# Mixer of a hybrid diffusion step: modulation weights loaded from ScalarE's queue, X and Y tables laid out by step, first inverses scattered earlier

## The reference, cut to what matters

```python
def gated_delta_chunked(q, k, v, g, beta, s0):
    ...
    a_mat = jnp.where(strict, jnp.einsum('bhnik,bhnjk->bhnij', kb, k) * decay, 0.0)
    rhs = jnp.concatenate([v * beta[..., None], kb * jnp.exp(gc)[..., None]], axis=-1)
    sol = lax.linalg.triangular_solve(a_mat + jnp.eye(CHUNK, dtype=jnp.float32), rhs,
                                      left_side=True, lower=True, unit_diagonal=True)
    ...
    def step(S, xs):
        u0_c, w_c, qk_c, qd_c, kd_c, gt_c = xs
        u = u0_c - jnp.einsum('bhck,bhkv->bhcv', w_c, S)
        o = jnp.einsum('bhck,bhkv->bhcv', qd_c, S) + jnp.einsum('bhij,bhjv->bhiv', qk_c, u)
        S = S * gt_c[..., None, None] + jnp.einsum('bhck,bhcv->bhkv', kd_c, u)
        return S, o
```

```python
def modulation(cond, w_ada_l, b_ada_l):
    m = jnp.einsum('nd,de->ne', cond, w_ada_l.astype(jnp.float32)) + b_ada_l.astype(jnp.float32)
    return jnp.split(m[:, None, :], 6, axis=-1)
```

## Time and profile before

| | us |
|---|---|
| median of 3 runs | 1893.29 |
| the runs | 1893.01 to 1895.04 |
| profiled execution, its own time | 1897.15 |
| its span in the profile | 1895.4 |
| busy in the span: PE, DVE, ACT, POOL | 1631.1, 1207.6, 932.4, 242.2 |

### The profile page before, as it was taken

The page is one execution under the profiler, slowest core; times in us unless marked ns, Lnnn a source line. Parts: engine busy times, 40 slices in busy tenths (PEclk is TensorE's granted clock), DMA queues, the critical chain, the costliest instruction groups (busy, mean ns, idle before and its releaser), DMA issues. The chain is left out here.

```text
span 1895.4 us, 32729 instructions
## 1 busy us (share of the span) xinstructions
PE 1631.1 (86%) x11909; PEld 1325.4 (70%) x11910; DVE 1207.6 (64%) x1728; ACT 932.4 (49%) x1438; POOL 242.2 (13%) x361
## 2 busy tenths in 40 slices
PE   3998886799895999999949989789979679999992
PEld 0798675687553888888838986678855468888881
DVE  1478453556346996996664883646654579899664
ACT  2254642233323886886543445323341278888651
POOL 0000035111000111111020000541200011111112
PEclk7899998999896999999969999879999889999996
DMA  8241356654305997997553110665331489999754
GB/s 339 78 151 48 100 153 163 189 178 143 137 34 205 412 405 294 380 408 269 211 218 112 56 48 1 174 197 157 95 129 53 167 304 402 408 397 409 296 198 178
DMA packets 186803, 392.96 MB, mean 207 GB/s; under 512 B 88682, under 2 KB 106114, under 8 KB 161094
## 3 DMA queue, kind: packets, MB, share of 16 engines
q1 hardware_dynamic: 163374, 326.12, 47.7%
q10 hardware_dynamic: 14824, 34.39, 4.6%
q0 software_dynamic: 8496, 30.94, 4.3%
HBM read 345.95 MB, written 45.45 MB: 207 GB/s over the span
## 5 line engine op out<-in xcount | busy, mean ns | idle before, releaser
L2363 DVE TENSOR_TENSOR expert_w_lo<-shared,expert_w_hi 128x2048 fp32r<-128x2048 f32 x192 | 433.4, 2287 | 58.3 <-ACT expert_w_hi L2302 58.3
L2302 ACT ACTIVATE expert_w_hi<-shared 128x2048 fp32r<-128x2048 f32 x192 | 366.5, 1913 | 44.1 <-PEq L146 39.6
L2229 PE MATMUL ps<-expert_w_hi,expert_x_hi 128*128 128x512 f32 x592 | 245.2, 414 | 11.0 <-DVE expert_x_lo L2358 9.2
L2231 PE MATMUL ps<-expert_w_hi,expert_x_lo 128*128 128x512 f32 x592 | 233.2, 394 | 0.0
L2230 PE MATMUL ps<-expert_w_lo,expert_x_hi 128*128 128x512 f32 x592 | 233.1, 394 | 0.0
L2229 PEld LDWEIGHTS ps<-expert_w_hi,expert_x_hi 128*128 128x128 f32 x592 | 113.5, 192 | 42.5 <-issue 12.9
L2231 PEld LDWEIGHTS ps<-expert_w_hi,expert_x_lo 128*128 128x128 f32 x592 | 112.3, 190 | 24.3
L2230 PEld LDWEIGHTS ps<-expert_w_lo,expert_x_hi 128*128 128x128 f32 x592 | 112.8, 191 | 18.7
L2284 PE MATMUL ps<-expert_w_hi,expert_hid_hi 128*128 128x512 f32 x296 | 115.8, 391 | 0.5 <-ACT expert_hid_hi L2337 0.5
L2199 POOL COPY expert_cur_idx<-slot_tokens 128x1 int32 x37 | 48.4, 1307 | 530.2 <-PE ps L2216 530.2
L2285 PE MATMUL ps<-expert_w_lo,expert_hid_hi 128*128 128x512 f32 x296 | 115.3, 390 | 0.0
(11 more groups left out here) (380 smaller groups left out, 3376.7 us busy)
## 6 DMA issues: line engine op xcount, KB each, us to landing
shared<-in_w_up SPq DMA_DIRECT2D x64, 1024.0 KB, 7.4
shared<-in_w_down SPq DMA_DIRECT2D x64, 1024.0 KB, 9.4
shared<-in_w_gate SPq DMA_DIRECT2D x64, 1024.0 KB, 8.3
qkv<-in_w_ada SPq DMA_DIRECT2D x20, 1280.0 KB, 6.1
shared<-in_w_in SPq DMA_DIRECT2D x10, 2048.0 KB, 9.2
y_table<-expert_y ACTq DMA_DIRECT2D x37, 512.0 KB, 8.5
qkvT<-in_w_ada SPq DMA_DIRECT2D x20, 768.0 KB, 8.5
setup_ada_ring<-in_w_ada SPq DMA_DIRECT2D x8, 1024.0 KB, 12.2
```

Source lines behind the costliest of these rows:

```text
L2229: pe.matmul(bank, x_hi[:, at], w_hi[:, j, w], start=(q == 0), stop=False)
L2231: return pe.matmul(bank, x_lo[:, at], w_hi[:, j, w], start=False, stop=(q == KD - 1))
L2302: act.activation(w_hi[:, j, :], raw[:, j, :], ACT.Copy).then_inc(w_hi_done, 1)
L2363: dve.tensor_tensor(w_lo[:, j, :], raw[:, j, :], w_hi[:, j, :].bitcast(F32), ALU.subtract).then_inc(w_lo_done, 1)
```

## The change

Four things change, all in the mixer.

- `load_after` is called by ScalarE at the end of `take(n)`, and no longer by SP. The loads of w_ada go to ScalarE's own DMA queue. Only the load of the first unit stays on SP.
- The tables base_x and base_y are laid out by step, both directions of a step side by side. `x_load` and `y_load` issue two loads of 128 KB each, not four of 64 KB.
- The tables corner and qk_table are laid out so that the two directions of a step can be addressed by one pattern: `bl_load` and `qk_load` issue one load, not two.
- `scatter(0)`, `x_load(0)` and `y_load(0)` come before `base_load(3)`; they came after it.

```diff
-    def load_after(self, sp, n):
+    def load_after(self, act, n):
 
         i = self.of_pair(n)
         if i is not None and i + 1 < len(self.todo):
-            sp.wait_ge(self.done, i + 1)
-            self.load(sp, i + 1)
+            act.wait_ge(self.done, i + 1)
+            self.load(act, i + 1)
...
+        def both(table, s, size):
+
+            a, b = (place(ORDER.index(t), d) for d, t in enumerate(tiles(s)))
+            return table[0:2 * NT * size].rearrange("(f x) -> f x", x=size)[a:b + 1:b - a]
...
+        def entry(table, at, n=1):
+
+            return table[at * BASE:(at + n) * BASE]
...
                 def bl_load(s):
                     sp.wait_ge(s_["t1l_p"], s)
-                    for d in range(2):
-                        sp.dma_start(flat(BtL)[half(d)], A.corner[place(s, d), half(d)]).then_inc(s_["bl_in"], 16)
+                    sp.dma_start(flat(BtL), both(A.corner, s, HB * DH * HB).rearrange("f (r n) -> f r n", r=HB)).then_inc(s_["bl_in"], 16)
...
-                    for d in range(2):
-                        sp.dma_start(QK[:, d].rearrange("p h n -> p (h n)"),
-                                     A.qk_table[place(s, d), :, d * DH * P:(d + 1) * DH * P]).then_inc(s_["qk_in"], 16)
+                    sp.dma_start(QK.rearrange("p d h n -> p d (h n)"), paired(both(A.qk_table, s, P * DH * P))).then_inc(s_["qk_in"], 16)
 
                 def scatter(i):
                     sp.wait_ge(s_["inv_done"], group(i) + 1)
                     p = rows_of(i)
                     for d in range(2):
-                        sp.dma_start(small(A.base_x, i, d), (Rt if d else R)[p, d]).then_inc(base_out[group(i)], 16)
-                        sp.dma_start(small(A.base_y, i, d), (R if d else Rt)[p, d]).then_inc(base_out[group(i)], 16)
+                        at = 2 * step_of(i, d) + d
+                        sp.dma_start(small(entry(A.base_x, at)), (Rt if d else R)[p, d]).then_inc(base_out[group(i)], 16)
+                        sp.dma_start(small(entry(A.base_y, at)), (R if d else Rt)[p, d]).then_inc(base_out[group(i)], 16)
 
                 def x_load(s):
...
-                    for d in range(2):
-                        for b in range(2):
-                            sp.dma_start(X[half(b), d], large(A.base_x, place(s, d), b)[:, d * DH:(d + 1) * DH]).then_inc(s_["xy_in"], 16)
+                    for b in range(2):
+                        sp.dma_start(eight_of(X, b), large(entry(A.base_x, 2 * s, 2), b)).then_inc(s_["xy_in"], 16)
...
                     if i + 1 < FRONT:
                         front_out(i + 1)
+                        if i == 2:
+                            scatter(0)
+                            x_load(0)
+                            y_load(0)
                         base_load(i + 1)
-                    units.load_after(sp, i)
-                    if i == 2:
-                        scatter(0)
-                        x_load(0)
-                        y_load(0)
                     units.store_after(sp, i)
                 for s in range(NT):
                     m = FRONT + PER * s
-                    units.load_after(sp, m)
                     if s < 2:
...
-                    units.load_after(sp, m + 1)
                     units.store_after(sp, m + 1)
...
                     act.wait_ge(s_["pt_p"], n + 1)
                     act.activation(pT[:, :, 0:nk], G.ps[:, 6:8, 0:nk], ACT.Copy).then_inc(s_["pt_taken"], 1)
+                    units.load_after(act, n)
```

More of the change, by code:

```diff
@@ L50 @@
 NB = P // SB
-BASE = 2 * 4 * 2 * (HB * HB + HB)
+BASE = 4 * 2 * (HB * HB + HB)
 BASE_PAD = 11 * P * 256
@@ L1149, in mixer_phase, with place, mine, small @@
         blocks = lambda b, c=0: G.ps[:, b, 256 * c:256 * (c + 1)].rearrange("p (h n) -> p h n", h=DH)
[L1151 to L1157, removed]
-            return of.rearrange("e (r n) -> r e n", n=HB)
+        def place(i, d):
+            g = group(i)
+            first, n = (0, 1, 3)[g], (1, 2, 2)[g]
+            return 2 * first + d * n + i - first
+        def both(table, s, size):
+            a, b = (place(ORDER.index(t), d) for d, t in enumerate(tiles(s)))
+            return table[0:2 * NT * size].rearrange("(f x) -> f x", x=size)[a:b + 1:b - a]
+        def mine(table, i, size):
+            return table[0:2 * NT * size].rearrange("(f x) -> f x", x=size)[place(i, 0):place(i, 1) + 1:place(i, 1) - place(i, 0)]
+        def entry(table, at, n=1):
+            return table[at * BASE:(at + n) * BASE]
+        def small(of):
+            of = of.rearrange("(q x) -> q x", x=SB * HB + SB)[:, 0:SB * HB]
+            return of.rearrange("q (r n) -> q r n", n=HB)[:, :, 0:SB]
+        def large(of, b):
+            of = of.rearrange("(e c x) -> e c x", c=2, x=HB * HB + HB)[:, b, 0:HB * HB]
+            return of.rearrange("e (r n) -> r e n", n=HB)
+        def step_of(i, d):
+            t = ORDER[i]
+            return NT - t if d and t else t
+        def paired(of):
+            return of.rearrange("f (p n) -> p f n", p=P)
         eight_of = lambda a, b: a[half(b)].rearrange("p d h n -> p (d h) n")
@@ L1176, in base_load @@
                         sp.wait_ge(s_["inv_done"], 1)
-                    sp.dma_start(V[rows_of(i), 0], small(A.base_b, i, 0)).then_inc(base_in[group(i)], 16)
-                    sp.dma_start(W[rows_of(i)], small(A.base_b, i, 1)).then_inc(base_in[group(i)], 16)
+                    sp.dma_start(V[rows_of(i), 0], small(entry(A.base_b, 2 * i))).then_inc(base_in[group(i)], 16)
+                    sp.dma_start(W[rows_of(i)], small(entry(A.base_b, 2 * i + 1))).then_inc(base_in[group(i)], 16)
                     if i:
@@ L1190, in bt_load @@
                     for d in range(2):
+                        i = ORDER.index(tiles(s)[d])
                         for b in range(2):
-                            sp.dma_start(Bt[half(b), d], large(A.base_b, place(s, d), b)[:, d * DH:(d + 1) * DH]).then_inc(s_["bt_in"], 16)
+                            sp.dma_start(Bt[half(b), d], large(entry(A.base_b, 2 * i + d), b)).then_inc(s_["bt_in"], 16)
                 def bl_load(s):
                     sp.wait_ge(s_["t1l_p"], s)
-                    for d in range(2):
-                        sp.dma_start(flat(BtL)[half(d)], A.corner[place(s, d), half(d)]).then_inc(s_["bl_in"], 16)
+                    sp.dma_start(flat(BtL), both(A.corner, s, HB * DH * HB).rearrange("f (r n) -> f r n", r=HB)).then_inc(s_["bl_in"], 16)
                 def qk_load(s):
@@ L1223, in y_load @@
                         sp.wait_ge(s_["yf_done"], at(s - 1, 1))
-                    for d in range(2):
-                        for b in range(2):
-                            sp.dma_start(Y[half(b), d], large(A.base_y, place(s, d), b)[:, d * DH:(d + 1) * DH]).then_inc(s_["xy_in"], 16)
+                    for b in range(2):
+                        sp.dma_start(eight_of(Y, b), large(entry(A.base_y, 2 * s, 2), b)).then_inc(s_["xy_in"], 16)
                 sp.dma_start(sinks[:, :], A.sink[l:l + 1, :].to_broadcast([P, NH])).then_inc(s_["par_in"], 16)
@@ L1264, in _ @@
                         sp.dma_start(A.new_state[0, l:l + 1].rearrange("a d h k v -> k (a d) h v"), S[:, 0]).then_inc(s_["s_out"], 16)
-                    units.load_after(sp, m + 2)
                     if s + 1 < NT:
@@ L1454, in _ @@
                             else:
-                                pe.wait_ge(s_["xy_in"], 128 * (s + 1))
+                                pe.wait_ge(s_["xy_in"], 64 * (s + 1))
                                 if s:
@@ L1481, in _ @@
                     if s:
-                        pe.wait_ge(s_["bl_in"], 32 * s)
+                        pe.wait_ge(s_["bl_in"], 16 * s)
                     for h in range(DH):
@@ L1519, in _ @@
                     if s:
-                        pe.wait_ge(s_["qk_in"], 32 * s)
+                        pe.wait_ge(s_["qk_in"], 16 * s)
                     if s + 1 == NT:
```

14 lines of the change are left out of this document (6 added, 8 removed).

## The result

The changed kernel takes 1916.67 us (median of 4 runs, 1912.5 to 1918.63) against 1893.15 us (4 runs), a ratio of 1.0119 [1.0101, 1.0138]: +22.5 us [19.1, 26.1], where the forecast was -4.3. The mixer of layer 0 went from 240.2 to 267.0 us (+26.8; forecast +12.2), that of layer 1 from 220.1 to 216.0 us (-4.1; forecast -17.5), both from SP's load of the sinks to its load of o_norm. So both layers miss in the same direction, by 14.6 and 13.4 us. Of layer 0's +26.8 us, TensorE's idle time in the mixer is 17.7 (64.0 against 46.3 us) and its busy time 9.1 (203.0 against 193.9), at a granted clock of 0.87 against 0.92.

What follows compares the result with a forecast made beforehand. TensorE's mixer was taken as a chain with holes, mostly waits for w_ada. Layer 0 +12.2 and layer 1 -17.5 gave -5.3 us, taken as -4.3: from 1893.3 to 1889.0 us, range 1879 to 1900.

Steps and rivals of the forecast that it cites:

- What bounds the kernel: Mixer: a chain on TensorE with holes; largest entry in layer 0 is waits for w_ada, 16.2 us in six.
- The first part: Tables by step, half the loads, earlier scatter(0): holes before steps close, -6.9 and -2.1 us in layer 0.
- bl_load and qk_load save one issue each. The bytes are the same: SP's table loads: one issue fewer for each of the two, with unchanged bytes; no cost given to the new layout.
- The second part: w_ada issued by ScalarE after take(n): later landings open holes in layer 0; pair 5 gains, -2.6 us there.
- the landing: Time from issue to arrival of w_ada's second half: 7.5 us for pairs 11, 14, 17; 9.1 for 6, 9, 10.
- The hole closes: Step 0 of layer 0: tables land at 290.1, before TensorE arrives at 291.0; -6.9 us and -2.1 of clock.
- Rival 3: Step 0: small stores ahead of the scatter cause the delay, so 3 to 4 us stay; 1896 us, chance 0.08.
- The clock: Behind new holes at pairs 9, 11, 14, 17 of layer 0 the granted clock falls: 2.0 us each, +8.0.
- rival 2: The clock stays up in layer 0's new holes of 3.3 to 3.7 us: 1881 us, chance 0.15.
- Rival 1: ScalarE starts the DMA only after the take ends, and every w_ada load takes 9.1 us: 1899 us, chance 0.22.
- Rival 4: Later w_ada loads don't show because TensorE arrives late anyway; layer 0's +25 us losses vanish: 1866 us, chance 0.05.
- pair 10's -2.0: Products of pair 10, layer 0: w_ada lands at 375.4 against 377.41, since SP was late there; -2.0 us.

Runs made afterwards that it cites:

- the best version: Changed kernel with corner table as before, pair 3's w_ada load by SP behind the Y loads, other loads on ScalarE once products free the buffer: 1864.72 us, 0.9823.
- both faults mended: Changed kernel with the corner table as before and pair 3's w_ada load issued by SP behind step 0's Y loads: ratio 0.9989.
- the version with 6.21 us before step 0: The best version, but pair 3's w_ada load also issued by ScalarE, behind exps of pair 3, not by SP: ratio 0.9852.
- the two-transfer corner version: Kernel before with only the corner table in its new layout, stored and loaded in two transfers of 64 rows each: ratio 0.9993.

## Why the prediction was wrong

**What bounds the kernel**: right in the main. In the mixer of layer 0, TensorE's idle time is 31.8, 46.3, 53.6 and 64.0 us in the best version, the kernel before, the one with both faults mended and the changed one, and the mixer takes 226.3, 240.2, 254.5 and 267.0. But single holes don't simply add up: the version with 6.21 us before step 0 has a mixer of layer 0 no longer than the best version's (223.3 us).

**The first part** was forecast at -9.0 (layer 0) and -5.4 (layer 1), together -14.4 us. It gave +2.5. With the corner table as before it gave -8.3, and the slow corner pattern by itself costs 11.0. The step that failed is "bl_load and qk_load save one issue each. The bytes are the same": I counted issues and bytes and took the transfer's duration as given. What is still missing from -14.4 lies nearly all in layer 0 (-1.7 us against -9.0): its hole did shrink, from 6.86 to 1.61 us, but TensorE then stood longer at pairs 3 and 5 for a w_ada that SP still issued at its old places. That is no fault of the sum, which had pair 5's load on ScalarE.

**The second part** was forecast at +21.2 and -12.1, together +9.1 us; measured alone +11.6 [7.8, 15.3]. That the total fits is partly luck: by itself this part lengthened the holes before step 0 by 4.0 and 4.8 us, which the sum doesn't have. In layer 1 this is the whole miss (-7.1 against -12.1). For the later pairs the mechanism holds. By pairs, forecast against the holes after: pair 6 6.7 and 7.58, pair 9 5.4 and 7.25, pair 10 5.35 and 5.21, pair 11 3.6 and 4.78, pairs 14 and 17 3.3 and 4.0 (0.73 of it was there before) against 5.52 and 4.36. Their sum is 28.4 against 34.7 us. The mis-sized term is the landing. The second half landed in 9.9, 10.9 and 8.9 us for pairs 6, 9 and 10, where I took 9.1, and in 8.7 and 9.5 for pairs 11 and 14, where I took 7.5: from the start of take(8) to the products of pair 9 were 368.30 - 356.88 = 11.4 us, not 9.5.

**Step 0** is where the forecast failed, for two reasons: the corner table, and pair 3's load. The chain of "The hole closes" against what came, in layer 0 (us):

| | forecast | changed kernel | both faults mended |
|---|---|---|---|
| scatters issued | 283.65 | 288.28 | 284.26 |
| X loads begin | 285.55 | 290.82 | 286.58 |
| Y loads issued | 288.15 | 295.06 | 290.15 |
| step 0 begins | 290.1 | 301.01 | 292.45 |

The last column rests on these lines:

```profile
283.44 0.82 SPq L1236 DMA_DIRECT2D base_y<-shared  x1
286.58 2.22 SPq L1243 DMA_DIRECT2D mixer_X<-base_x  x2
288.84 1.31 SPq L1249 DMA_DIRECT2D mixer_Y<-base_y  x2
```

```profile
292.45 1.97 PE L1423 MATMUL ps<-mixer_X,mixer_NTb 64*64 64x64 f32 x32 [1.04 <-issue]
```

Of the 10.9 us that the changed kernel was late, 4.6 had come about when the scatters were out (SP behind the corner stores, then one issue of 3.00 us where I had taken 0.5), and 4.1 came with the last landing: 5.95 us, where I had taken 1.9 from 297.85 - 295.96, a stretch with little other traffic (DMA share 0.33 from 296.00 to 297.80 us before, 1.08 from 295.06 to 301.01 after); the rest came with the issues between. I wrote "What I count on is that w_ada no longer sits ahead of the small stores in SP's queue", and priced the load of pair 3 by what it does to itself (0.5 us), not by what it does to step 0's tables. Rival 3 was near: it had the hole stay, but for the stores' sake. With both omissions mended the change measured -2.1 us [-4.4, 0.0] against my -4.3, so nothing large is missing from the total besides them; by layers it is +14.4 and -14.4 where the sum had +12.2 and -17.5. The rule of the Trainium skill that I had put beside the sum ("DMA: Bandwidth & Descriptors", section "Issuing engines are not separate DMA queues") bears exactly on this place. I had applied it to pairs 11, 14 and 17 alone; the X and Y landings (8.3 us beside w_ada, 2.8 ahead of it) agree with it.

**The clock**: right for the sum, but the length of the hole alone does not decide it (last point of this document). Stretches after, behind pairs 9, 11, 14 and 17 (the clock is the third number from the end), answer to the earlier trace rows:

```profile
368.30:373.30 5.00, 5.00 (x76) 4.00 (x77) 0.00 (x0) 0.00 (x0) 0.00 (x0) 0.50 0.03 8
...
406.40:411.40 5.00, 4.99 (x76) 4.00 (x77) 0.56 (x4) 0.00 (x0) 2.51 (x4) 0.52 0.01 3
447.30:452.30 5.00, 4.93 (x76) 3.94 (x77) 0.52 (x3) 0.00 (x0) 2.71 (x4) 0.51 0.02 3
485.90:490.90 5.00, 4.97 (x82) 4.06 (x82) 0.86 (x4) 0.00 (x0) 0.00 (x0) 0.66 0.02 3
```

So rival 2 fell. By length times (1 - clock), as in the forecast, the four cost at most 2.5, 2.4, 2.5 and 1.7 us, 0.8 of it 7.3, against the 8.0 forecast. **Rival 1** named slower, half for another reason: ScalarE's issue was not late against the take's start, but its second condition, 9.1 us for every load, came about (8.7 to 10.9). It had nothing for step 0, and its 1899 us was too small for what came. Rival 4's 1866 doesn't follow from its +25 us (1889.0 - 25 = 1864); with pair 10's -2.0 counted, the losses are 23.3 us.

**The interval** of 1879 to 1900 held no case in which step 0 got worse, since I allowed the hole only to close or to stay in part.

## What to carry to other kernels

A large load on a second queue has no place in the first queue's order: before moving it, list every small transfer that is issued within its flight, and who waits for those; where one matters, put the large load on the same queue behind it. Issue a load where its buffer becomes free, not at the next convenient instruction of the engine: that alone was 31 us here, all of it in the layer whose units follow each other closely. And a merged transfer is judged by its patterns, not by its number of issues: look at the outermost size on both sides.

## What the runs showed of the hardware that I had not expected

- A 128 KB store whose memory side has 2 outermost kept two DMA engines busy (share 0.13) and held SP 5.1 us; two stores of 64 KB landed in 2.5 us each.
- The 128 KB loads of X and Y landed in 2.8 to 3.4 us ahead of a 2 MB load of the other queue, and in 6.4 to 9.0 us beside it.
- The clock's fall isn't decided by the hole's length alone: products behind holes of 2.39 and 2.81 us took 1.30 us in the two-transfer corner version, but 2.36 us behind one of 1.73 us in the version with pair 3's load on ScalarE.
